# A two-pass reload of expert results, split last weights and a residual reload by tile

## The reference

```python
g_idx = top-1 of the 4 group probabilities
e_top_v, e_top_i = lax.top_k(e_sel, 2)                  # 2 of the group's 8 experts
weights = softmax(e_top_v) * g_top_p
global_idx = g_idx * 8 + e_top_i                        # two of the 32 experts
hid = silu(t @ w_gate[e]) * (t @ w_up[e]) * combine     # width 256
ffn = sum over the two experts of hid @ w_down[e]
out = layer_norm(2 ** 0.25 * h1 + ffn, ln2_g, ln2_b)
```

## Time and profile before

| what | value |
|---|---|
| median of 3 runs | 432.66 us (432.59 to 433.03) |
| profiled execution | 433.34 us, span of its instructions 431.5 us |
| PE busy | 408.7 us, 95% of the span |
| DVE busy | 186.9 us, 43% |
| ACT busy | 114.3 us, 26% |
| POOL busy | 83.5 us, 19% |
| DMA moved | 139.11 MB, mean 322 GB/s |

### The profile page before, as it was taken

How to read it: one execution, slowest core, us unless ns; L and a number is a source line. 1 busy time by engine, 2 the same in 40 slices (tenths; PEclk the granted TensorE clock), 3 DMA queues, 4 the chain that set the end, 5 groups by cost and what they waited for, 6 DMA issues and landing times.

```text
span 431.5 us, 6632 instructions
## 1 busy us (share of the span) xinstructions
PE 408.7 (95%) x2578; PEld 276.5 (64%) x2578; DVE 186.9 (43%) x368; ACT 114.3 (26%) x185; POOL 83.5 (19%) x113
## 2 busy tenths in 40 slices
PE   7999999999999999999999999999999997888783
PEld 6888877888888888956556555655555564453331
DVE  2479622499957467864312222221222121211077
ACT  3542376973122002310111111111111110103111
POOL 2220000000000001123233323332332331200124
PEclk9999999999999999999999999999999998999998
DMA  8876531221369999999999999999999999999684
GB/s 264 263 196 198 172 95 28 94 97 22 115 214 419 425 420 420 420 362 396 416 414 414 418 409 416 412 414 414 415 418 417 416 418 416 419 420 417 253 342 195
DMA packets 37377, 139.11 MB, mean 322 GB/s; under 512 B 5107, under 2 KB 17427, under 8 KB 25062
## 3 DMA queue, kind: packets, MB, share of 16 engines
q1 hardware_dynamic: 31184, 126.89, 74.3%
q0 software_dynamic: 6144, 11.84, 7.8%
q10 hardware_dynamic: 22, 0.02, 0.1%
HBM read 134.41 MB, written 12.58 MB: 341 GB/s over the span
## 4 chain that ended last, share of the span: by engine, by line
PE 82%; DMA 11%; SPq 4%; DVE 1%; issue 1%; ACT 0%; DVEq 0%; POOLq 0%
PE bank L1104 21%; PE bank L917 12%; PE bank L919 12%; PE bank L918 12%; PE bank L1133 10%; DMA wgu_first<-in_exp_w_up 6%; PE bank L1094 3%; PE bank L1202 2%; PE bank L1124 2%; SPq L509 2%; DMA xg<-h_rows,x_rows 2%; DMA pair_y<-y_pairs 1%; PE bank L1014 1%; PE bank L900 1%; DMA y_pairs<-ys,y_rows 1%; DMA raw<-in_w_in 1%
## 5 line engine op out<-in xcount | busy, mean ns | idle before, releaser
L1104 PE MATMUL bank<-wgu,xTg 128*64 128x256 f32 x736 | 86.2, 388 | 5.8 <-DMA wgu<-in_exp_w_up 4.8
L1104 PEld LDWEIGHTS bank<-wgu,xTg 128*64 128x64 f32 x736 | 52.0, 139 | 32.6 <-DMA wgu<-in_exp_w_up 5.5
L917 PE MATMUL bank<-xT_hi,w_hi 128*128 128x512 f32 x160 | 63.5, 397 | 0.8 <-DVE xT_lo L1244 0.8
L919 PE MATMUL bank<-xT_hi,w_lo 128*128 128x512 f32 x160 | 62.8, 393 | 0.0
L918 PE MATMUL bank<-xT_lo,w_hi 128*128 128x512 f32 x160 | 62.8, 392 | 0.0
L1544 DVE TENSOR_TENSOR hid<-gated,bank 64x256 f32<-64x256 f32 x32 | 13.5, 423 | 106.8 <-ACT gated L843 106.7
L683 POOL DMA_INDIRECT y_pairs<-ys,y_rows x32 | 32.5, 1015 | 135.5 <-PE bank L1094 103.9
L843 ACT ACTIVATE gated<-bank 64x256 f32<-64x256 f32 x32 | 12.1, 377 | 129.1 <-PE bank L1104 129.1
L1133 PE MATMUL bank<-wdn,hidT 128*64 128x512 f32 x192 | 45.3, 593 | 0.0
L1221 DVE TENSOR_TENSOR w_lo<-raw,w_hi 128x2048 fp32r<-128x2048 f32 x12 | 27.5, 2288 | 26.9 <-ACT w_hi L757 26.9
L678 POOL DMA_INDIRECT xg<-h_rows,x_rows x31 | 31.4, 1014 | 24.8 <-issue 8.3
(11 more groups left out here) (252 smaller groups left out, 496.7 us busy)
## 6 DMA issues: line engine op xcount, KB each, us to landing
wgu<-in_exp_w_gate SPq DMA_DIRECT2D x24, 1024.0 KB
wgu<-in_exp_w_up SPq DMA_DIRECT2D x24, 1024.0 KB
wdn<-in_exp_w_down SPq DMA_DIRECT2D x24, 1024.0 KB
raw<-in_w_in SPq DMA_DIRECT2D x9, 1024.0 KB, 6.0
raw<-in_w_out SPq DMA_DIRECT2D x4, 1024.0 KB, 5.1
wdn_extra<-in_exp_w_down SPq DMA_DIRECT2D x4, 1024.0 KB
wgu_spare<-in_exp_w_gate SPq DMA_DIRECT2D x4, 1024.0 KB
wgu_spare<-in_exp_w_up SPq DMA_DIRECT2D x4, 1024.0 KB
```

The costliest lines, as they stand in the source:

```text
L917: pe.matmul(dst, a_hi, b_hi, start=start, stop=False)
L919: return pe.matmul(dst, a_lo, b_hi, start=False, stop=stop)
L1104: mm = pe.matmul(psum[2 + b][BLOCK * which:BLOCK * which + BLOCK, 0:F], xTg[b][:, j, h * BLOCK:(h + 1) * BLOCK], wgu[s][:, which, k, :], s ...
```

## The change

Four things change.

- **Results by expert number.** DVE works out `swapped`, 1 where a token's first choice has the higher expert number, and moves the places (`y_put`) so that the result of the lower-numbered expert stands in the first half of `y_pairs`. The two weights are swapped to match. `hot_y` is made later in DVE's list.
- **First ones ahead of the last scatter.** Expert 31 can never be the lower of two, so SP's loads of k = 0 wait for all scatters but expert 31's, and those of k = 1 for that one too. The eight loads now go (0,0), (1,0), (2,0), (3,0), (0,1), (1,1), (2,1), (3,1), and PE adds in the order: k = 0 of all four tiles, then k = 1 of tiles 1, 2, 3.
- **Gate/up weights of expert 31 in three pieces.** Each of gate and up comes in rows k 0 to 3, 4 to 5 and 6 to 7 with a semaphore per piece, and PE starts on the first.
- **h1 by tile.** The one 2 MB transfer becomes four of 512 KB, and PE waits for each tile's own.

```diff
+LAST_PIECES = ((0, 4), (4, 6), (6, 8))
...
+            def refill_last_gu():
+                e = N_EXP - 1
+                sp_.wait_ge(gu_summed, used_by(e, 0) + 1)
+                for n, (k0, k1) in enumerate(LAST_PIECES):
+                    for which, w in enumerate((exp_w_gate, exp_w_up)):
+                        sp_.dma_start(gu_place(slot_of(e), which)[:, k0 * F:k1 * F], gu_of(w, e)[:, k0 * F:k1 * F]).then_inc(gu_last_in[n], 16)
...
-            sp_.dma_start(h1[:, :, :].rearrange("p t (a h) -> p t a h", a=2),
-                          h1_rows.rearrange("(t p a) h -> p t a h", p=P, a=2)).then_inc(h1_in, 16)
+            for t in range(TT):
+                sp_.dma_start(h1[:, t, :], h1_rows[2 * t * P:2 * (t + 1) * P, :].rearrange("(p a) h -> p (a h)", a=2)).then_inc(h1_in[t], 16)
...
-            for b in range(1, ROWS):
-                sp_.wait_ge(y_scattered[b], mains(b))
-            for t in range(TT):
-                for k in range(TOP_K):
+            for k in range(TOP_K):
+
+                for b in range(1, ROWS):
+                    sp_.wait_ge(y_scattered[b], mains(b) - (16 if k == 0 and b == (N_EXP - 1) % ROWS else 0))
+                for t in range(TT):
                     src = y_pairs[2 * (k * T + t * P):2 * (k * T + (t + 1) * P), :]
                     sp_.dma_start(pair_y[t][k][:, :], src.rearrange("(p a) h -> p (a h)", a=2)).then_inc(pairs_in[t][k], 16)
...
+            def gate_up_last():
+                i = N_EXP - 1
+                pe.wait_ge(xTg_ready, i + 1)
+                pe.wait_ge(hid_ready, i - 1)
+                for n, (k0, k1) in enumerate(LAST_PIECES):
+                    pe.wait_ge(gu_last_in[n], 32)
+                    mm = gate_up_part(slot_of(i), i % 2, range(k0, k1))
                 mm.then_inc(gu_summed, 1)
...
-            pe.wait_ge(h1_in, 16)
             pe.wait_ge(diag_ready, 1)
             for t in range(TT):
+                pe.wait_ge(h1_in[t], 16)
...
-            for t in range(TT):
-                last = 0 if t < DVE_ADDED else TOP_K - 1
-                for k in range(last + 1):
+            for k in range(TOP_K):
+                for t in range(DVE_ADDED if k else 0, TT):
+                    last = 0 if t < DVE_ADDED else TOP_K - 1
                     pe.wait_ge(pairs_in[t][k], 16)
...
-            v.tensor_tensor(hot_y[:, :, :], pairs(chosen[:, :, :, :]), per_pair(y_place, N_EXP), ALU.mult).then_inc(hot_ready, 1)
+
+            def put_by_expert():
+
+                link(v.tensor_tensor(swapped[:, 0, :], chosen_e[:, 0, :], chosen_e[:, 1, :], ALU.is_gt))
+                step(v.scalar_tensor_tensor(out=y_put[:, 0:TT], in0=swapped[:, 0, :], scalar=2.0 * T, in1=y_place[:, 0:TT], op0=ALU.mult, op1=ALU.add))
+                link(v.scalar_tensor_tensor(out=y_put[:, TT:], in0=swapped[:, 0, :], scalar=-2.0 * T, in1=y_place[:, TT:], op0=ALU.mult, op1=ALU.add))
+                v.tensor_tensor(hot_y[:, :, :], pairs(chosen[:, :, :, :]), per_pair(y_put[:, :], N_EXP), ALU.mult).then_inc(hot_ready, 1)
...
             copy_first_T(1, xTg_ready)
+            put_by_expert()
...
-                link(v.reciprocal(weight[:, 0, :], wsum[:, :]))
-                v.tensor_tensor(weight[:, 1, :], weight[:, 0, :], vexp[:, :], ALU.mult).then_inc(weights_ready, 1)
+                link(v.reciprocal(by_choice[:, 0, :], wsum[:, :]))
+                step(v.tensor_tensor(by_choice[:, 1, :], by_choice[:, 0, :], vexp[:, :], ALU.mult))
+                step(v.tensor_scalar(kept[:, 0, :], swapped[:, 0, :], -1.0, 1.0, ALU.mult, ALU.add))
+                link(v.tensor_copy(swapped[:, 1, :], swapped[:, 0, :]))
+                link(v.tensor_copy(kept[:, 1, :], kept[:, 0, :]))
+                step(v.tensor_tensor(kept[:, :, :], kept[:, :, :], by_choice[:, :, :], ALU.mult))
+                link(v.tensor_tensor(swapped[:, :, :], swapped[:, :, :], by_choice[:, :, :], ALU.mult))
+                for k in range(TOP_K):
+                    v.tensor_tensor(weight[:, k, :], kept[:, k, :], swapped[:, 1 - k, :], ALU.add).then_inc(weights_ready, 1)
```

More of the change, by code:

```diff
@@ L143, in hybrid_moe_layer @@
         weight = sb("weight", [P, TOP_K, TT])
+        by_choice = sb("by_choice", [P, TOP_K, TT])
+        swapped = sb("swapped", [P, TOP_K, TT])
+        kept = sb("kept", [P, TOP_K, TT])
+        y_put = sb("y_put", [P, TOP_K * TT])
         iota_f = sb("iota_f", [P, 140])
@@ L292, in hybrid_moe_layer @@
         dn_in = [sem(f"dn_in{s}") for s in range(RING)]
+        gu_last_in = [sem(f"gu_last_in{n}") for n in range(len(LAST_PIECES))]
         over_gu_in = sem("over_gu_in")
@@ L371, in hybrid_moe_layer @@
         pairs_in = [[sem(f"pairs_in{t}_{k}") for k in range(TOP_K)] for t in range(TT)]
-        h1_in = sem("h1_in")
+        h1_in = [sem(f"h1_in{t}") for t in range(TT)]
         diag_ready = sem("diag_ready")
@@ L565, in _ @@
                     refill_dn(head + u, r)
+            def refill_last_gu():
[4 more added lines that the diff above has]
+                        sp_.dma_start(gu_place(slot_of(e), which)[:, k0 * F:k1 * F], gu_of(w, e)[:, k0 * F:k1 * F]).then_inc(gu_last_in[n], 16)
             for q in range(head + turns * RING, N_EXP):
-                if q + 1 < N_EXP:
+                if q + 2 < N_EXP:
                     refill_gu(q + 1, 0)
+                elif q + 2 == N_EXP:
+                    refill_last_gu()
                 refill_dn(q, 0)
@@ L858, in make_diagonals @@
                 act.activation(diag[:, 0, :], ident[:, :], ACT.Copy, scale=ALPHA).then_inc(diag_ready, 1)
-                act.wait_ge(weights_ready, 1)
+                act.wait_ge(weights_ready, TOP_K)
                 for t in range(TT):
@@ L1095, in turn_x, with gate_up_part @@
                 mm.then_inc(xg_turned, 1)
[L1097 to L1101, removed]
+            def gate_up_part(s, b, ks):
+                for k in ks:
                     h, j = divmod(k, 4)
@@ L1106, in gate_up @@
                                        start=k == 0, stop=k == KT - 1)
+                return mm
+            def gate_up(i, s, b, lag, loads):
+                pe.wait_ge(gu_in[s], 32 * loads)
+                pe.wait_ge(xTg_ready, i + 1)
+                wait_free(pe, hid_ready, i, lag)
+                gate_up_part(s, b, range(KT)).then_inc(gu_summed, 1)
+            def gate_up_last():
+                i = N_EXP - 1
+                pe.wait_ge(xTg_ready, i + 1)
+                pe.wait_ge(hid_ready, i - 1)
+                for n, (k0, k1) in enumerate(LAST_PIECES):
+                    pe.wait_ge(gu_last_in[n], 32)
+                    mm = gate_up_part(slot_of(i), i % 2, range(k0, k1))
                 mm.then_inc(gu_summed, 1)
@@ L1158, in pe_item @@
                     return
-                gate_up(q + r * RING, slot_of(q), q % 2, 2, loads_of(q, r))
+                if static(r) and q == N_EXP - 1:
+                    gate_up_last()
+                else:
+                    gate_up(q + r * RING, slot_of(q), q % 2, 2, loads_of(q, r))
                 if q == 1:
@@ L1515, in match_over @@
                 v.tensor_tensor(over_x_hot[:, :, :], over_match[:, :, :], per_pair(x_place, MAX_OVER), ALU.mult).then_inc(over_hot_ready, 1)
-                v.tensor_tensor(over_y_hot[:, :, :], over_match[:, :, :], per_pair(y_place, MAX_OVER), ALU.mult).then_inc(over_hot_ready, 1)
+                v.tensor_tensor(over_y_hot[:, :, :], over_match[:, :, :], per_pair(y_put[:, :], MAX_OVER), ALU.mult).then_inc(over_hot_ready, 1)
             def find_over():
```

## The result

The changed kernel took 436.11 us (median of 7 runs, 434.17 to 437.02), the kernel before 432.7 us (7 runs): ratio 1.0068, interval 1.0044 to 1.0091, by that ratio about 2.9 us slower (the two medians are 3.4 us apart). The forecast was 434.8 us, slower; its range ended at 436.2, so the first median lies just inside it. The profiled execution took 436.53 us with a span of 434.8 us, 3.3 us more than the earlier trace rows.

The account below looks back on a forecast made before the run. DVE was taken as practically the bound of the tail: 415.1 + 1.52 + 3 x 3.28 + 7.21 = 433.7 against 431.52, +2.15 us on the 432.66 median, giving 434.8 us; range 432.9 to 436.2.

Parts of the forecast that it names:

- `gate_up(31)` unbroken from 391.4 to 395.0: Expert 31's gate/up products on PE: with weights in pieces, 3.6 us of work ends at 395.0 instead of 397.0.
- `down(30)` at 396.1, released by DMA: Expert 30's down products wait for their weights, starting 0.75 us earlier than 396.85; 1.25 of PE's 2 us are lost.
- Down 31 lands at 398.6, before `down(31)` would start at 398.86: Expert 31's down weights arrive before PE needs them, so both last scatters are issued 0.75 us earlier.
- The release at 405.46: First k = 0 load, after expert 30's scatter issued at 399.4 takes 6.0 us; 1.7 us earlier than before.
- Fifth load 9.6 us after the first issue: DVE's load `pair_y[0][1]`, formerly second in the queue, now fifth, lands at 415.0.
- DVE 2.6 us late: DVE's tail starts at 415.1 instead of 412.49, waiting for its own load; all statistics, normalisation and stores stand behind.
- 0.46 us won in DVE's waits for PE: In DVE's tail: 2 x 0.15 us between tiles and 0.16 in the last statistics, the most PE's gain gives.
- Part 2: h1 by tile: PE's sums of h1 start 2.4 us earlier, near 401.5; a gain for PE alone.
- Part 4: Routing work for results by expert number: hidden under other waits, taken as 0, up to 0.3 us if cover is gone.
- Rival A: No change: expert 30's scatter takes 4.19 us, loads run right behind `ln2b`; +0.4 us, 433.1 us; chance 0.18.
- Rival B: Faster: PE, not DVE, sets the tail if the fifth load lands by 412.9; -0.9 us, 431.7 us; chance 0.10.
- C: Expert 30's scatter takes the whole 7.3 us: release 406.7, DVE at 416.4; +3.5 us, 436.1 us; chance 0.12.

Follow-up runs that it names:

- the order alone: Kernel before with only the eight loads and PE's additions reordered k by k, all loads still waiting for all scatters: 436.55 us, ratio 1.0088.
- the series of places: Time from first load issue to DVE's start across kernels: its load second, about 5.0 to 5.6 us; third 6.3; fifth 9.5 to 9.9; fourth not run.
- part 3 undone: Changed kernel with the old release and order of the eight loads and of PE's additions: 432.27 us, ratio 0.9994.
- pieces: Kernel before with only the last gate/up weights in three pieces: 433.95 us, ratio 1.004.
- routing alone: Kernel before with only the results by expert number, loads and PE order as before: 433.5 us, ratio 1.0016.
- pieces again: Second run of the kernel before with only the last gate/up weights in three pieces: 433.09 us, ratio 1.0022.
- one ahead: Changed kernel with only load (0,0) ahead of expert 31's scatter, then (0,1), (1,0) and so on, PE adding tile by tile: 432.09 us, ratio 0.9971.

## Why the prediction was right, and where its sizes were off

The mechanism was right, and it decided: the load that DVE's list asks for first moved from second to fifth place. Shown by the order alone (1.0088), by undoing it (0.9994), and by the series of places.

Term by term, measured in the first profile:

- *`gate_up(31)` unbroken from 391.4 to 395.0:* 391.59 to 395.26. Right. *`down(30)` at 396.1, released by DMA:* 396.43. Right; 1.16 us of PE's lead goes here.
- *"Down 31 lands at 398.6, before `down(31)` would start at 398.86", so both scatters 0.75 earlier.* Wrong. `down(31)` waited 0.81 us for its weights, to 399.61, so expert 31's scatter gained nothing; expert 30's gained 0.38. I had room of 0.26 us between landing and use, and the landing came about 1 us later than I worked out: the two down weights, 1 MB each, were 3.18 us apart (396.43 to 399.61), where I had counted 2.50. In the other kernels with pieces they were 3.0 to 3.2 apart; why is open.
- *The release at 405.46*, 1.7 us before that of the profile before. It came at 406.26, 0.94 before: 0.4 by the later issue, 0.4 because expert 30's scatter took 6.46 us, not 6.0 (between 5.7 and 7.2 in the other runs with an early release). In the second profile of the same kernel it came at 405.38, so a reading of one profile is not sure to better than some 0.9 us.
- *Fifth load 9.6 us after the first issue.* 9.9, and 9.5 to 9.8 in the others. Right; the first profile was at the upper end.
- *DVE 2.6 us late.* 3.7: 0.8 from the release and 0.3 from the fifth load. This is the term that the forecast had too small; in the second profile DVE was 2.42 us late (414.91).
- *PE ends its last product before 422.* 422.84; DVE never waited for it.
- *0.46 us won in DVE's waits for PE, 18.57 from DVE's start to the end.* 18.6, and 19.0 before. Right.
- *Part 2 is for PE alone.* 1.7 us earlier (2.4 forecast, with PE at 401.5 instead of 402.25), and the end did not move: 1.0014. *Part 4 nothing:* 1.0016, not clear of no change.
- *Rival A*, expert 30's scatter in 4.19 us: not seen; 5.7 to 7.2. *Rival B*, PE sets the tail: even with DVE's wait gone the kernel stayed at 1.002. *C*, a scatter of 7.3: seen only in the kernel in which DVE takes an early load (399.44 to 406.65, 7.2), though the first set's median, 436.11, is its time.

What the early release gained was at most about 1.2 us, against 3.6 lost by the order. By the Trainium skill's rule for a GpSimd DMA (DMA: Bandwidth & Descriptors, section Anatomy of one DMA) a scatter takes an estimated 2.6 us; the last two scatters took 3.05 at the shortest, in the kernel with the order alone, and 7.2 at the longest.

## What to carry to other kernels

Before releasing loads earlier by reordering them, look at which load the consumer's in-order list asks for first, and count its new place in the queue: from the second place to the fifth it lost 4.2 to 5.0 us here, about 1.5 us a place, more than the release gained. Split a late transfer only when what is queued behind it is not needed next: PE ran ahead by 1.8 us and gave nearly all of it back in waits for the two transfers behind. A mild form of the idea, with only the one load that PE's first tile needs ahead, avoided the price; whether it gains is not settled (0.9971 in one set; 0.999 without the pieces in another).

## What the runs showed of the hardware

**The last scatter landed just after the stream ahead of it.** Issuing it earlier did not bring it earlier. Landings of `ln2b`, the last of the stream, by issue plus time to landing; here the rows of part 3 undone, of the pieces (the same in both profiles), of routing alone and of the order alone with the late release:

```profile
ln2b<-in_ln_b SPq DMA_DIRECT2D x1, 512.0 KB, 15.4
```

```profile
ln2b<-in_ln_b SPq DMA_DIRECT2D x1, 512.0 KB, 15.6
```

```profile
ln2b<-in_ln_b SPq DMA_DIRECT2D x1, 512.0 KB, 14.9
```

```profile
ln2b<-in_ln_b SPq DMA_DIRECT2D x1, 512.0 KB, 14.4
```

| kernel | ln2b issued + time = landed | last scatter issued | first load after all scatters | scatter to load |
|---|---|---|---|---|
| before | 392.17 + 14.6 = 406.8 | 402.95 | 407.20 | 4.25 |
| part 3 undone | 390.38 + 15.4 = 405.8 | 401.40 | 406.23 | 4.83 |
| pieces | 390.41 + 15.6 = 406.0 | 401.45 | 406.44 | 4.99 |
| pieces again | 390.65 + 15.6 = 406.3 | 401.63 | 406.62 | 4.99 |
| routing alone | 390.49 + 14.9 = 405.4 | 401.62 | 405.82 | 4.20 |
| order alone, late | 390.22 + 14.4 = 404.6 | 402.88 | 405.93 | 3.05 |

In the first five the load is issued 0.4 us after `ln2b` landed, whatever the scatter's issue (4.2 to 5.0 us before it). In the last the clock's fall in `gate_up(31)` (5.36 us) made the scatter late, the stream was through first, and the scatter took its own 3.05 us. H1 by tile alone is like it, with the same 5.36 and 402.79 to 406.12, 3.33 us; its profile has no landing of `ln2b`. The Trainium skill says something that fits: a completion is an ordered write, which lands only after every earlier write of the same DMA engine, across its queues (DMA: Bandwidth & Descriptors, section Queues, rings and completion order); these rows agree with it, with their 0.4 us, but do not show that mechanism, since no run moved `ln2b`. And expert 30's scatter does not follow `ln2b`. In one ahead the rows are

```profile
399.07 0.99 POOL L699 DMA_INDIRECT y_pairs<-ys,y_rows  x1 [6.04 <-ACT ys L866]
...
ln2b<-in_ln_b SPq DMA_DIRECT2D x1, 512.0 KB, 13.3
```

It was issued 5.67 us after `ln2b` (393.40) and had landed by 404.96, when the first load went out, 1.7 us before `ln2b` (406.7); the last scatter of the same kernel landed at 407.04. So being issued behind `ln2b` is not enough to be held by it. If the last scatter is held by it, what ends the loop is the 1 MB of `ln2g` and `ln2b` in front, not PE. That was not tried.

**The clock.** In the kernel before, executions with a mean granted clock below 0.986 had a median of 434.1 us, the others 432.1 (24 and 72 executions, the three sets of the experiments together). The cut at 0.986 is mine, and it doesn't carry over to the kernels with the order k by k: there PE ends longer before the end, and after PE's last product the clock is at half, which lowers the mean. In the one profile with such a fall in the sums of h1 PE had stood 3.16 us before it; in the second profile with the same wait it did not fall. Where h1 comes in one transfer (before, pieces, routing) 36 of 132 executions were below 0.986; where it comes by tile, with the loads tile by tile, 1 of 60. That PE's wait for h1 is what lets the clock fall fits this but is not shown, and h1 by tile alone was no faster (1.0014). That spread of 2 us is as large as the effects sought, and is why a single execution here decides nothing.
